# Norms of a two-layer encoder kernel: sums of squares spread by a ones matrix and inverse roots taken as exp(-0.5 ln), in place of one-column sums, square root, reciprocal and diagonal matrix

## The reference

```python
def rmsnorm(x, g):
    y = x * lax.rsqrt(jnp.mean(x * x, axis=-1, keepdims=True) + 1e-6)
    return y * g
def l2norm(x):
    return x * lax.rsqrt(jnp.sum(x * x, axis=-1, keepdims=True) + 1e-6)

# x: (512 tokens, 1024)
# layer 0: h = rmsnorm(x); one projection feeds
#   gated DeltaNet, 4 heads of 128: q = l2norm(q) * 128**-0.5, k = l2norm(k),
#     chunked delta rule, o_a = rmsnorm(o, g) * silu(gate)
#   differential attention, 4 heads: o_b = rmsnorm(softmax1 v - lam * softmax2 v, g) * (1 - lam_init)
#   x = x + concat(o_a, o_b) @ w_out
# layer 1: h = rmsnorm(x); banded attention, 16 heads of 64, learned bias; x = x + o @ w_out
# each layer then: h = rmsnorm(x); x = x + (silu(conv3(h @ w_gate)) * (h @ w_up)) @ w_down
# out = rmsnorm(x)
```

## Time and profile before

| | us |
|---|---|
| median of three runs (lowest, highest) | 1537.61 (1536.41, 1541.71) |
| the profiled execution: its own time | 1534.61 |
| its span, from the first to the last instruction | 1532.9 |
| PE busy | 1467.8 (96%) |
| DVE busy | 827.1 (54%) |
| ACT busy | 589.4 (38%) |
| POOL busy | 140.6 (9%) |

### The profile page before, as it was taken

One profiled execution on the slowest core, in us unless ns is written; L12 is line 12 of the kernel. 1 busy time (PEld: TensorE's weight loads), 2 busy tenths in 40 slices (PEclk: granted clock), 3 DMA queues, 4 the chain that ended last, 5 costly groups with the idle time before them and its releaser, 6 DMA issues.

```text
span 1532.9 us, 19662 instructions
## 1 busy us (share of the span) xinstructions
PE 1467.8 (96%) x6775; PEld 1145.8 (75%) x6775; DVE 827.1 (54%) x1209; ACT 589.4 (38%) x791; POOL 140.6 (9%) x149
## 2 busy tenths in 40 slices
PE   5979898899989999999999999999999999999996
PEld 4768878666677888888888666666678888888875
DVE  5676675565565665346555444444374664356543
ACT  4423232244444543233344444444344443223342
POOL 1040051000121100000012000000030000000011
PEclk9989989999999999999999999999999999999998
DMA  7321101011324632333224222212131322333221
GB/s 203 118 55 28 42 15 42 1 42 55 110 83 117 177 111 81 92 110 96 75 86 112 82 60 66 56 54 74 56 110 55 109 75 86 113 107 85 79 86 55
DMA packets 218640, 124.78 MB, mean 81 GB/s; under 512 B 6048, under 2 KB 215435, under 8 KB 218341
## 3 DMA queue, kind: packets, MB, share of 16 engines
q1 hardware_dynamic: 213744, 112.54, 26.0%
q0 software_dynamic: 3664, 11.58, 2.7%
q10 hardware_dynamic: 1188, 0.08, 0.1%
HBM read 119.94 MB, written 9.48 MB: 84 GB/s over the span
## 4 chain that ended last, share of the span: by engine, by line
PE 89%; DVE 5%; ACT 2%; issue 2%; DMA 1%; POOL 1%; SPq 0%; DVEq 0%; ACTq 0%; POOLq 0%
PE acc L570 25%; PE acc L572 23%; PE acc L571 23%; PE R L796 5%; PE R L671 4%; PE R L827 4%; PE R L812 1%; PE R L609 1%; DVE cta L1295 1%; ACT wh L359 1%; PE R L669 1%; DMA xin<-in_x 1%; DVE ml L1248 0%; PE R L802 0%; DVE wl L363 0%
## 5 line engine op out<-in xcount | busy, mean ns | idle before, releaser
L570 PE MATMUL acc<-mh,wh 128*128 128x512 f32 x1120 | 467.2, 417 | 9.1 <-DVE ml L1248 4.9
L572 PE MATMUL acc<-mh,wl 128*128 128x512 f32 x1120 | 441.2, 394 | 0.0
L571 PE MATMUL acc<-ml,wh 128*128 128x512 f32 x1120 | 441.0, 394 | 0.0
L363 DVE TENSOR_TENSOR wl<-raw,wh 128x2048 fp32r<-128x2048 f32 x116 | 265.9, 2292 | 141.5 <-ACT wh L359 141.5
L359 ACT ACTIVATE wh<-raw 128x2048 fp32r<-128x2048 f32 x116 | 221.1, 1906 | 168.9 <-PE acc L572 167.7
L570 PEld LDWEIGHTS acc<-mh,wh 128*128 128x128 f32 x1120 | 212.7, 190 | 88.8 <-issue 43.5
L572 PEld LDWEIGHTS acc<-mh,wl 128*128 128x128 f32 x1120 | 212.7, 190 | 46.1
L571 PEld LDWEIGHTS acc<-ml,wh 128*128 128x128 f32 x1120 | 213.2, 190 | 39.8 <-issue 3.6
L570 PE MATMUL acc<-ah,wh 128*128 128x512 f32 x352 | 139.1, 395 | 0.0
L572 PE MATMUL acc<-ah,wl 128*128 128x512 f32 x352 | 138.8, 394 | 0.0
L571 PE MATMUL acc<-al,wh 128*128 128x512 f32 x352 | 138.8, 394 | 0.0
(11 more groups left out here) (272 smaller groups left out, 1607.6 us busy)
## 6 DMA issues: line engine op xcount, KB each, us to landing
raw<-in_ffn_w_in SPq DMA_DIRECT2D x88, 512.0 KB, 5.0
raw<-in_even_w_in SPq DMA_DIRECT2D x24, 512.0 KB, 5.3
raw<-in_ffn_w_out SPq DMA_DIRECT2D x32, 384.0 KB, 4.1
raw<-in_ffn_w_out SPq DMA_DIRECT2D x32, 320.0 KB, 3.7
raw<-in_odd_w_qkv SPq DMA_DIRECT2D x16, 512.0 KB, 4.5
rel_bias_extended<-rel_bias_rows POOLq DMA_DIRECT2D x16, 320.0 KB, 4.0
raw<-in_even_w_out SPq DMA_DIRECT2D x8, 512.0 KB, 4.5
raw<-in_odd_w_qkv SPq DMA_DIRECT2D x16, 256.0 KB, 3.1
```

What stands on the lines that cost most here:

```text
L363: nc.vector.tensor_tensor(wl[s][:, :], raw[s][:, :], wh[s][:, :].bitcast(F32), ALU.subtract).then_inc(sem(f"w_tail{s}"), 1)
L570: nc.tensor.matmul(o, ah_, bh_, start=first, stop=False)
L571: nc.tensor.matmul(o, ah_, bl_, start=False, stop=False)
L572: return nc.tensor.matmul(o, al_, bh_, start=False, stop=last)
```

## The change

Each column path is replaced by this: the squares themselves are multiplied by the ones matrix, so that every partition has the whole sum of each token along 512 columns; ACT then takes `Ln` of sum plus epsilon (128x512, out of PSUM) and `Exp` with scale -0.5 in SBUF. The factors 1/D and 1/P go into the scale of `Square`. Norm 4 stays as a column, and norm 0 too. The core of the diff, with line numbers left out:

```diff
+            def inverse_root(to, phase, name, i, done):
+                r = full(act, phase, name, i)
+                free(A(to, r[:, :], ACT.Ln, bias=epsc[:, :]), phase, name, i)
+                read(act, phase, name, i)
+                A(to, to, ACT.Exp, scale=-0.5).then_inc(sem(done), 1)
 # PE, dn_pair
-                for h in (0, 1):
-                    pe.wait_ge(sem(f"sqk{h}"), p + 1)
-                    r = job("dn", f"sq_c{h}", p)
-                    token_sums(r, 0, d[h]["sqq"])
-                    done(token_sums(r, NB, d[h]["sqk"]), "dn", f"sq_c{h}", p)
+                spread("rk", "sqk", "sqk")
                 for h in (0, 1):
                     pe.wait_ge(sem(f"gbc{h}"), p + 1)
                     each("grow", h, d[h]["gbc"], triu)
...
-                spread("rk", "sqk", "dk")
-                step("kk", "kh", "kh", ["rk"])
-                spread("rq", "sqq", "dq")
-                step("qk", "kh", "qh", ["rq"])
+                step("kk", "kh", "kh", need=[("kn", p + 1)])
+                spread("rq", "sqq", "sqq")
+                step("qk", "kh", "qh", need=[("qn", p + 1)])
...
-                for h in (0, 1):
-                    pe.wait_ge(sem(f"sqo_dn{h}"), p + 1)
-                    r = job("dn", f"oc{h}", p)
-                    done(token_sums(r, 0, d[h]["sqo"]), "dn", f"oc{h}", p)
-                spread("ro", "sqo", "do")
+                spread("ro", "sqo", "sqo_dn")
 # ACT, dn_pair
                 for h in (0, 1):
-                    r = full(act, "dn", f"sq_c{h}", p)
-                    free(A(nr[h][:, 0:2, :], r[:, 0:2 * NB]..., ACT.Sqrt, bias=epsc[:, :]), "dn", f"sq_c{h}", p)
+                    inverse_root(d[h]["sqk"], "dn", f"rk{h}", p, f"ik{h}")
...
+                for h in (0, 1):
+                    inverse_root(d[h]["sqq"], "dn", f"rq{h}", p, f"iq{h}")
                 copy_out("At", "At", p)
...
-                    free(A(nr[h][:, 4, :], r[:, 0:NB], ACT.Sqrt, bias=epsc[:, :], scale=1.0 / P), "dn", f"oc{h}", p)
+                    inverse_root(d[h]["sqo"], "dn", f"ro{h}", p, f"io{h}")
 # ACT, differential attention
-                    A(osd[:, :], r[:, :], ACT.Square).then_inc(sem("sqo_diff"), 1)
-                    r = full(act, ph, "oc", i)
-                    free(A(nq[:, 0, :], r[:, 0:NB], ACT.Sqrt, bias=epsc[:, :], scale=1.0 / P), ph, "oc", i)
+                    A(osd[:, :], r[:, :], ACT.Square, scale=P ** -0.5).then_inc(sem("sqo_diff"), 1)
+                    settled(act, is_full(ph, "ro", i))
+                    free(A(osd[:, :], R[2][:, :], ACT.Ln, bias=epsc[:, :]), ph, "ro", i)
+                    settled(act, is_read(ph, "ro", i))
+                    A(osd[:, :], osd[:, :], ACT.Exp, scale=-0.5).then_inc(sem("io_diff"), 1)
                     next(evac, 0)
                     next(evac, 0)
-                    settled(act, is_full(ph, "ro", i))
-                    free(A(osd[:, :], R[2][:, :], ACT.Copy, scale=sub8[:, :]), ph, "ro", i)
 # DVE, differential attention
-                    read(dve, ph, "oc", i)
-                    V.reciprocal(nq[:, 1, :], nq[:, 0, :]).then_inc(sem("inv_od"), 1)
-                    dve.wait_ge(sem("inv_od"), i + 1)
-                    V.tensor_tensor(blk(osd[:, :]), rows(ident), cols(nq[:, 1, :]), ALU.mult)...
                     next(evac, 0)
-                    read(dve, ph, "ro", i)
-                    free(V.tensor_tensor(osb[:, :], r[:, :], osd[:, :], ALU.mult), ph, "pv", i)
+                    dve.wait_ge(sem("io_diff"), i + 1)
+                    free(V.scalar_tensor_tensor(out=osb[:, :], in0=r[:, :], scalar=sub8[:, :], in1=osd[:, :],
+                                                op0=ALU.mult, op1=ALU.mult), ph, "pv", i)
 # PE, norms 1 to 3: norm_sums(n) goes, and norm_rows(n) moves four steps ahead to its place
-                        norm_sums(norm)
-                        run(first, 4)
                         norm_rows(norm)
 # ACT, norms 1 to 3
-            norm_roots(1)
+            inverse_root(rstd[:, :], "norm1", "row", 0, "rstd")
```

More of the change, by code:

```diff
@@ L101 @@
 XT_JOBS = [(f"x{k}", k % 4) for k in range(KD)]
-NORM_JOBS = [("col", 1), ("row", 0)]
+NORM_JOBS = [("row", 0)]
+LAST_JOBS = [("col", 1)]
 AB_JOBS = [("abT", 2), ("ab", 3)]
@@ L462, in sum_squares @@
                 if norm > 1:
-                    read(pool, f"norm{norm - 1}", "col", 0)
+                    full(pool, f"norm{norm - 1}", "row", 0)
                 pool.memset(ssum[:, :], 0.0).then_inc(sem("ssum"), 1)
@@ L505, in _ @@
                     e = d[h]
-                    read(pool, "dn", f"rq{h}", p)
+                    pool.wait_ge(sem(f"qn{h}"), p + 1)
                     read(pool, "dn", f"grow{h}", p)
@@ L618, in norm_rows @@
             def norm_rows(n):
-                pe.wait_ge(sem("diag"), n + 1)
+                if n:
+                    pe.wait_ge(sem("ssum"), 9 * n + 9)
+                else:
+                    pe.wait_ge(sem("diag"), 1)
                 r = job(f"norm{n}", "row", 0)
-                done(nc.tensor.matmul(r[:, :], ones, sq[0][:, :], start=True, stop=True), f"norm{n}", "row", 0)
+                done(nc.tensor.matmul(r[:, :], ones, (ssum if n else sq[0])[:, :], start=True, stop=True),
+                     f"norm{n}", "row", 0)
             pe.wait_ge(sem("cst_in"), 16)
@@ L1212, in _ @@
             out_proj(UNIT["out0"], 1)
-            norm_roots(1)
+            inverse_root(rstd[:, :], "norm1", "row", 0, "rstd")
             mlp(0, 2, False)
-            norm_roots(2)
+            inverse_root(rstd[:, :], "norm2", "row", 0, "rstd")
             each4(feat_evac("odd", UNIT["odd"]))
@@ L1220, in _ @@
             out_proj(UNIT["out1"], 3)
-            norm_roots(3)
+            inverse_root(rstd[:, :], "norm3", "row", 0, "rstd")
             mlp(1, 4, True)
@@ L1231, in norm_rstd @@
             def norm_rstd(n):
+                if n in (1, 2, 3):
+                    dve.wait_ge(sem("rstd"), n)
+                    return
                 if n:
-                    read(dve, f"norm{n}", "col", 0)
+                    read(dve, "norm4", "col", 0)
                 else:
                     dve.wait_ge(sem("root0"), 1)
-                V.reciprocal(rcol[:, :], sdc[:, :]).then_inc(sem("rstd"), 1)
-                dve.wait_ge(sem("rstd"), n + 1)
-                if n == 4:
+                V.reciprocal(rcol[:, :], sdc[:, :]).then_inc(sem("rcol"), 1)
+                dve.wait_ge(sem("rcol"), 2 if n else 1)
+                if n:
                     return
                 V.tensor_tensor(blk(sq[0][:, :]), rows(ident), cols(rcol[:, :]), ALU.mult).then_inc(sem("diag"), 1)
-                r = full(dve, f"norm{n}", "row", 0)
-                free(V.tensor_copy(rstd[:, :], r[:, :]), f"norm{n}", "row", 0)
-                read(dve, f"norm{n}", "row", 0)
+                r = full(dve, "norm0", "row", 0)
+                free(V.tensor_copy(rstd[:, :], r[:, :]), "norm0", "row", 0)
+                read(dve, "norm0", "row", 0)
             def x_tail(norm, k):
@@ L1367, in dn_pair @@
                     e = d[h]
-                    read(dve, "dn", f"sq_c{h}", p)
-                    own(V.reciprocal(nr[h][:, 2:4, :], nr[h][:, 0:2, :]), f"inv{h}", p + 1)
-                    V.tensor_tensor(blk(e["sqk"]), rows(ident), cols(nr[h][:, 3, :]), ALU.mult)\
-                        .then_inc(sem(f"dk{h}"), 1)
-                for h in (0, 1):
-                    e = d[h]
                     r = full(dve, "dn", f"gcol{h}", p)
@@ L1387, in dn_pair @@
                     e = d[h]
-                    r = full(dve, "dn", f"rk{h}", p)
-                    free(V.tensor_tensor(e["kh"], r[:, :], e["kT"], ALU.mult), "dn", f"rk{h}", p)
-                    V.tensor_tensor(blk(e["sqq"]), rows(ident), cols(nr[h][:, 2, :]), ALU.mult)\
-                        .then_inc(sem(f"dq{h}"), 1)
+                    dve.wait_ge(sem(f"ik{h}"), p + 1)
+                    V.tensor_tensor(e["kh"], e["sqk"], e["kT"], ALU.mult).then_inc(sem(f"kn{h}"), 1)
                 for h in (0, 1):
@@ L1489, in dn_pair @@
                     e = d[h]
-                    read(dve, "dn", f"oc{h}", p)
-                    own(V.reciprocal(nr[h][:, 5, :], nr[h][:, 4, :]), f"inv_o{h}", p + 1)
-                    V.tensor_tensor(blk(e["sqo"]), rows(ident), cols(nr[h][:, 5, :]), ALU.mult)\
-                        .then_inc(sem(f"do{h}"), 1)
-                for h in (0, 1):
-                    e = d[h]
-                    r = full(dve, "dn", f"ro{h}", p)
+                    dve.wait_ge(sem(f"io{h}"), p + 1)
                     dve.wait_ge(sem(f"gC_full{h}"), p + 1)
-                    free(V.tensor_tensor(e["on"], r[:, :], e["gC"], ALU.mult), "dn", f"ro{h}", p)
-                    read(dve, "dn", f"ro{h}", p)
+                    own(V.tensor_tensor(e["on"], e["sqo"], e["gC"], ALU.mult), f"on{h}", p + 1)
                     dve.wait_ge(sem("x_kept"), 16)
```

35 lines of the change are left out of this document (12 added, 23 removed), and 2 rows, old and new, of the table _DN.

## The result

| | before | changed |
|---|---|---|
| median (lowest to highest), same chip | 1539.32 (1536.41 to 1541.71, 4 runs) | 1563.82 (1559.39 to 1567.76, 4 runs) |
| profiled execution, span | 1532.9 | 1566.1 |
| PE busy | 1467.8 | 1460.2 (93%) |
| ACT busy | 589.4 | 627.2 (40%) |

The ratio is 1.0169, 95% interval 1.0144 to 1.0193. The forecast was 1562 us in a range from 1547 to 1573. PE has less to do and the kernel is slower: it waits.

A forecast was written before the change was run, and what follows sets the result against it. The prediction took PE as the bound (89% of the chain of waits), with ACT's time on the path where roots fall. Terms summed to +24.9 us on 1534.61, 1559.5; with 3.0 us to the median, 1562 us, range 1547 to 1573.

The forecast's parts named there:

- first pair to its output's squares: First DeltaNet pair: PE idling ahead of kk (1.5 us for both pairs) and q's later second root (+2.75 us).
- end of the first pair: Output roots delay Silu, wh, wl and gbc on ACT and DVE, so PE's next grow starts later: +2.8 us.
- end of the second pair, with the clock in the first head: First scores 2.6 us later behind the output roots, plus 1.2 us from PE starting at half clock: +3.8 us.
- three boundaries: Between differential heads: ns 3.75 us later each, plus new half clock less old spells: +13.9 us, largest and least certain.
- last head: Last differential head, no wh and wl between: root chain of 3.87 us in place of sums, wait and copy: +0.8 us.
- norms 1 to 3 and all behind: Norms 1 to 3 lose their column sums on PE, roots standing beside a projection: -3.4 us.
- The half clock behind a boundary: PE idles over 6 us between differential heads, so the clock falls at all three boundaries: 2.2 us each.
- q's roots: Both DeltaNet pairs: PE's second qk waits for the second q root, +2.75 us each, +5.5 us for two.
- the spell at `kk`: PE idles about 3 us ahead of kk, clock may fall: 1.5 us for both pairs, between 0 and 5.
- Absorbed tail: Rival: ns is not what PE waits for between differential heads, so +13.9 becomes 0: +11 us, 1549; chance 10%.
- One load serves both: Rival: Ln and Exp share a table, a root takes 1.31 us: -3.6 us, 1534, no change; chance 7%.
- PE's column work bounds: Rival: roots hide fully and PE sheds its column sums and waits: -23 us, 1514; chance 5%.

The follow-up runs named there:

- e2: Kernel before with only the differential heads in the new form: 1556.41 us, ratio 1.0130.
- e3: Kernel before with only the DeltaNet head pairs in the new form: 1555.81 us, ratio 1.0124.
- e5: Changed kernel with Identity in place of Ln in every new root, same tiles and order, most root table loads gone: 1539.50 us, ratio 1.0018.
- e7: Changed kernel with the weight tile's split (wh) ahead of Ln and Exp on ACT in the differential heads: 1547.96 us, ratio 1.0072.
- e1: Kernel before with only norms 1 to 3 in the new form: 1532.44 us, ratio 0.9970.
- e6: Changed kernel with 21 idle 128x128 products on PE behind the spread of each of the first three differential heads: 1556.20 us, ratio 1.0133.
- e10: Changed kernel with Abs_reciprocal_sqrt in place of Ln and Exp, and the weight split ahead of the root in the differential heads: 1516.91 us, ratio 0.9865.
- e4: The changed kernel run again as it stands: 1562.63 us, ratio 1.0177 against the kernel before.
- e8: Changed kernel with both heads' Ln side by side, then both Exp, in the DeltaNet pairs: 1557.07 us, ratio 1.0132.
- e11: Changed kernel with the edits of e7 and e8 together, Ln and Exp kept: 1548.41 us, ratio 1.0074.
- e9: Changed kernel with the one function Abs_reciprocal_sqrt in place of Ln and Exp: 1531.97 us, ratio 0.9973.
- e12: Ln and Exp in norms 1 to 3 and in differential heads with the split first, DeltaNet pairs keeping their columns: 1534.10 us, ratio 0.9985.

## Why the prediction was right, and where it was not

| term of the forecast | forecast | between the two profiles |
|---|---|---|
| first pair to its output's squares (half of 1.5, and 2.75) | +3.5 | +6.7 |
| end of the first pair | +2.8 | +2.4 |
| second pair to its output's squares | +3.5 | +4.9 |
| end of the second pair, with the clock in the first head | +3.8 | +3.7 |
| three boundaries | +13.9 | +19.4 |
| last head | +0.8 | +1.0 |
| norms 1 to 3 and all behind | -3.4 | -5.0 |
| sum | +24.9 | +33.2 |

**Direction, places and mechanism held.** 56 executed table loads became 71, 15 more, in twos around tiles of 128x512; the second `qk` came 2.95 us later behind its spread (2.7 forecast), `ns` 10.6 us behind the end of the spread (some 10 forecast, 4.2 before; from its start it is 11.6), the clock fell at all three boundaries of the profiled execution, and no wait at `kk` was over 4 us (3.3). e2 and e3 show that both kinds of heads carry the slowdown, e5 and e7 that it hangs on the loads and on what stands behind them, e1 that the norms gain what their sums cost.

**The half clock behind a boundary was mis-sized.** I took 2.2 us from the spell at the start of the first pair. e6 measures 3.9 us each. The waits were right: 3.75 us forecast, 4.0 us in e6. With those, 3 x 4.0 + 3 x 3.9 less 4.1 us makes 19.6 against the measured 19.4; the 4.1 are what the falls of the kernel before made heads 2 and 3 longer than head 1 (2.8 us, and 1.3 once head 3 is taken as 3.4 us shorter by its work, as it is in e6 and e10). PE works at 0.50 for about 9 us here, not 4 to 5. A spell's length at one place was no measure for another.

**The half clock behind the second `qk` was missing.** q's roots were priced as a wait of 2.75 us (measured from the spread to the second `qk`: 8.4 - 5.5, 2.95 us), the spell at `kk` as 0.75 us per pair (measured from `grow` to q's spread: 1.5), and the text went on with "PE runs almost without a wait from there", which leaves out the clock. From the second `qk` to the output's squares it is 86.1 us in the first pair where it was 83.4, 2.8 us more. Of 3.2 us that half clock took there, 1.7 lie behind `qk`, from 111 to 115 us: all seven profiles with `Ln`, `Exp` and their loads in the pairs have such a spell between 107 and 116 us (the changed kernel, e3, e4, e6, e7, e8, e11), and none of the other seven has. The other 1.5 us, from 193 to 197, are not the roots': they stand at PE's wait of 2.5 us for the state `st`, which the kernel before has too, and e1, whose pairs are unchanged, has a spell there as well and 1.1 us more than before up to the squares. Without the loads (e5) the stretch from the first `qk` to the squares is within 0.6 us of before.

**The sum fitted better than its terms.** Between the two profiles the terms are 8 us short (+24.9 against +33.2); between the medians nothing is missing (+24.5). The two profiled executions lie on opposite sides of their medians, before 4.7 us under, changed 3.9 us over, and the mean granted clock was 0.966 in the profiled execution of the changed kernel and 0.970 in the two fastest of its four. So an ordinary execution has less half clock than the one the terms are compared with, and half clock is what the forecast had too low. The hit at 1562 is in part luck.

**The rivals.** *Absorbed tail*: refuted, 19.5 us of waits at `nm`. *One load serves both*: not so in this build, by the 19 and 19 loads of 1283 ns. Its price would be about that of e5, which has the tiles and next to no loads: 1539.5 us where I had 1534. The Trainium skill (ScalarE: Activation LUTs, Table sets) has a set that holds both functions, one load for the two; no run here shows it in use. The drain of 1.38 us per switch that the Trainium skill gives in ScalarE: Activation LUTs (What ACT_TABLE_LOAD costs) did not show either: load and function stand 0.02 us apart. *PE's column work bounds*: wrong for the changed kernel and nearly right as a price. I said 1514 us once ACT's chain is under 3.0 us; e9 has a chain of 2.0 us and stood at 1532, because `wh` behind the root belongs to the chain as well, and e10, with `wh` out of it, is at 1516.9.

## What to carry to other kernels

Price a chain of ACT functions by its table loads first: here two loads of 1.28 us stood around 1.3 us of work, and a version with one function, and the weight split ahead of it, turned a loss of 1.7% into a gain of 1.4%. Where a step on ACT grows, look at what is queued behind it (here the split of a weight tile that DVE and then PE wait for), and move that first. A new wait of PE can cost twice: its length, and the half clock behind it, which at the boundaries of the profiled execution was as much again. The length of the wait alone does not give that second price: half clock took 3.4 us behind waits of 4.0 us (e5), 6.8 behind 4.5 (e9), 5.1 behind 6.6 (the changed kernel), from nothing to 5.1 behind 2.7 (e7, e11, e12) and nothing behind 1.0 (e10).

## What was not expected of the hardware

- Idle products in PE's wait did not slow the kernel but made its median 6 us lower (e6, within overlapping intervals): 4.85 us of products whose result is overwritten kept the clock at 1.00 and made each of three boundaries 3.9 us shorter in the profile.
- Stretches at half clock lasted less than 4 us behind `qk` (111 to 115 us) and about 10 us at a boundary (350.5 to 360.7 us), in one execution.
- `Abs_reciprocal_sqrt` out of PSUM took 0.69 us on 128x512, the same as `Ln`, and two heads in a row needed one load (e9, q's roots at 103.32 and 104.88 us, no load between).
